# Thirteen modulation tiles folded on VectorE and moved to later stages, and a recurrence interleaved unit by unit

## The reference

```
m_x = silu(c) @ w_mod + b_mod            # six vectors of 1024: shift, scale, gate, shift, scale, gate
hx  = rmsnorm(x, g1) * (1 + m_x[1]) + m_x[0]
px  = hx @ w_in                           # columns rx, rg, u, v, gr, gg
xr  = dwconv1d(px.rx)                     # the same for the context
for direction in (forward, backward):     # bidirectional linear recurrence, 1280 channels
    r, i  = sigmoid(xr @ wa + ba), sigmoid(xr @ wx + bx)   # block-diagonal weights
    log_a = -8 * r * softplus(-lam);  a = exp(log_a)
    b     = sqrt(-expm1(2 * log_a)) * (i * xr)
    h_t   = a_t * h_(t-1) + b_t            # the context first, its last state starts the tokens
y_r = gelu(px.rg) * (h_fwd + h_bwd)
y_g = gelu(px.u) * (w_s @ rmsnorm(gelu(px.v)) + b_s)
x   = x + m_x[2] * ((sig(px.gr) * (y_r @ w_pr) + sig(px.gg) * (y_g @ w_pg)) @ w_out)
h2  = rmsnorm(x, g2) * (1 + m_x[4]) + m_x[3];  x = x + m_x[5] * conv_ffn(h2)
```

## Time and profile before

| | us |
|---|---|
| median of 3 runs | 3241.24 |
| lowest and highest | 3238.25, 3242.54 |
| profiled execution, its time | 3241.85 |
| its span, first to last instruction | 3240.0 |
| PE busy in the span | 3171.5 (98%) |
| DVE busy | 2060.2 (64%) |
| ACT busy | 1248.9 (39%) |
| mean granted TensorE clock | 0.993 |

### The profile page before, as it was taken

How to read it: one execution, slowest core, us unless ns; L and a number is a source line. 1 busy time by engine, 2 the same in 40 slices (tenths; PEclk the granted TensorE clock), 3 DMA queues, 4 the chain that set the end, 5 groups by cost and what they waited for, 6 DMA issues and landing times.

```text
span 3240.0 us, 37547 instructions
## 1 busy us (share of the span) xinstructions
PE 3171.5 (98%) x14084; PEld 2513.9 (78%) x14084; DVE 2060.2 (64%) x3455; ACT 1248.9 (39%) x2295; POOL 425.9 (13%) x186
## 2 busy tenths in 40 slices
PE   8999999999999999999999999999999999999999
PEld 7877778878778656767778888888888888888887
DVE  7678354367898899546646896777761455555554
ACT  4365222233223322235433335999982211111111
POOL 0000000014132000000002444333334000000000
PEclk9999999999999999999999999999999999999999
DMA  5243324332242454221122444676867555555553
GB/s 211 59 126 124 102 71 146 121 109 95 72 155 84 143 172 134 72 79 52 59 91 95 133 139 137 176 206 193 219 177 231 205 187 190 188 189 190 187 190 115
DMA packets 285845, 455.77 MB, mean 141 GB/s; under 512 B 148952, under 2 KB 156248, under 8 KB 285280
## 3 DMA queue, kind: packets, MB, share of 16 engines
q1 hardware_dynamic: 150560, 409.84, 37.9%
q10 hardware_dynamic: 135104, 43.52, 6.0%
HBM read 372.01 MB, written 81.26 MB: 140 GB/s over the span
## 4 chain that ended last, share of the span: by engine, by line
PE 91%; DVE 6%; ACT 1%; issue 1%; DMA 0%; POOL 0%; ACTq 0%; DVEq 0%
PE psum L644 91%; DVE wl L1489 1%; ACT wh L1077 1%; DVE yb L1701 0%; DVE psum L1865 0%; DVE trig L1584 0%; DVE lb L1692 0%; DVE st L1942 0%; DVE cs L1699 0%; DVE y L1703 0%; DVE trig L1587 0%; DVE trig L1586 0%; DVE trig L1589 0%; DVE trigw L1588 0%; DVE trigw L1585 0%
## 5 line engine op out<-in xcount | busy, mean ns | idle before, releaser
L644 PE MATMUL psum<-h_hi,wh 128*128 128x512 f32 x2144 | 857.0, 400 | 32.7 <-DVE h_lo L1633 13.2
L1489 DVE TENSOR_TENSOR wl<-ring,wh 128x1024 fp32r<-128x1024 f32 (+2 forms) x322 | 375.7, 1171 | 747.4 <-ACT wh L1077 746.4
L644 PE MATMUL psum<-h_lo,wh 128*128 128x512 f32 x2144 | 849.2, 396 | 0.0
L644 PE MATMUL psum<-h_hi,wl 128*128 128x512 f32 x2144 | 849.2, 396 | 0.0
L1077 ACT ACTIVATE wh<-ring 128x1024 fp32r<-128x1024 f32 (+2 forms) x492 | 504.6, 1027 | 813.5 <-PE psum L644 789.3
L2235 POOL TENSOR_TENSOR wl<-ring,wh 128x1024 fp32r<-128x1024 f32 x170 | 423.0, 2489 | 1784.3 <-ACT wh L1077 1784.3
L644 PEld LDWEIGHTS psum<-h_hi,wh 128*128 128x128 f32 x2144 | 406.4, 190 | 133.1 <-issue 40.6
L644 PEld LDWEIGHTS psum<-h_hi,wl 128*128 128x128 f32 x2144 | 405.8, 189 | 95.8
L644 PEld LDWEIGHTS psum<-h_lo,wh 128*128 128x128 f32 x2144 | 406.3, 190 | 88.5 <-issue 1.7
L644 PE MATMUL psum<-ews_hi,wh 128*128 128x512 f32 x1024 | 404.1, 395 | 0.7 <-ACT ga L1456 0.7
L644 PE MATMUL psum<-ews_hi,wl 128*128 128x512 f32 x1024 | 404.0, 395 | 0.0
(11 more groups left out here) (384 smaller groups left out, 3776.6 us busy)
## 6 DMA issues: line engine op xcount, KB each, us to landing
ring<-tables SPq DMA_DIRECT2D x256, 512.0 KB, 3.6
acts_scratch<-ga SPq DMA_DIRECT2D x128, 256.0 KB, 2.2
gates_scratch<-stage ACTq DMA_DIRECT2D x8, 4096.0 KB, 26.2
abuf<-acts_scratch SPq DMA_DIRECT2D x128, 256.0 KB, 3.8
gbuf<-gates_scratch SPq DMA_DIRECT2D x128, 256.0 KB, 4.0
ring<-w_up SPq DMA_DIRECT2D x44, 512.0 KB, 3.6
ring<-w_modb SPq DMA_DIRECT2D x32, 512.0 KB, 3.6
ring<-w_moda SPq DMA_DIRECT2D x16, 512.0 KB, 5.6
```

Of the source, the lines that this page charges most:

```text
L644: return nc.tensor.matmul(out, lhsT, rhs, start=first, stop=last, **kw)
L1489: TT(wl, slot(t, 0, size[t]), wh.bitcast(F32), ALU.subtract).then_inc(S("low_by_ve"), 1)
```

## The change

1. modb14 to modb26 leave the gates. They follow u0 to u6 and pg0 to pg5, one behind each (`FOLDED`). DVE folds each in its ring slot: it multiplies the 8 chunks by silu(c) and adds the chunks up in three steps (1024, 512, 256 and 128 columns), and PE does one matmul of the folded 128x128 chunk with ones, 16 columns, instead of eight. 14 tiles stay with the gates. The modulation of the second half (`a2`) is finished before the first `x_mixed`.
2. In the stages v, u, gg, map and pg, `high_after` and `low_after` look R = 5 tiles ahead instead of 3, at most three weight parts as before.
3. The recurrence: DVE's two steps for lq and la become one, in place (la = (la + 1) * lw, `loss_ready`), and ACT forms 1 - la (`decay_of`, Identity, 768 columns). DVE's groups are dissolved: after the scans of unit n come the last multiplication of unit n + 4 (`scale_input`) and the first two of unit n + 5 (`unit`).
4. Semaphores of the stage f and of iota are merged; no instruction of computation is added or removed there.

```diff
-MODB_LATE = 27
-MODB = [MODB_LATE * n // (2 * NR) for n in range(2 * NR + 1)]
+MODB_FOLD, MODB_LATE = 14, 27
+MODB = [MODB_FOLD * n // (2 * NR) for n in range(2 * NR + 1)]
+FOLDED = {f"u{n}": MODB_FOLD + n for n in range(7)} | {f"pg{n}": MODB_FOLD + 7 + n for n in range(6)}
...
+            def folded_modulation(name):
+                if name in FOLDED:
+                    k = FOLDED[name]
+                    pe.wait_ge(S("mod_folded"), k - MODB_FOLD + 1)
+                    mm(mods[:, k - MODB_FOLD, :], wchunk(TILE[f"modb{k}"], 0), ones[:, 0:MS], True, True)\
+                        .then_inc(PE, 1)
...
-            def high_after(t):
-                while next_high[0] < len(WHOLE_OF) and WHOLE_OF[next_high[0]] <= t + RH:
+            def high_after(t, ahead=RH):
+                while next_high[0] < len(WHOLE_OF) and WHOLE_OF[next_high[0]] <= t + ahead:
+                    if ahead > RH and WHOLE_OF[next_high[0] - RH] > t:
+                        break
...
+            def decay_of(n):
+                act.wait_ge(S("loss_ready"), n + 1)
+                A(la[:, n % 5, :], la[:, n % 5, :], ACT.Identity, scale=-1.0, bias=ones[:, 0:1])\
+                    .then_inc(S("a_ready"), 1)
...
+                if j:
+                    decay_of(n - 1)
                 wait(act, S("lru_done"), n - 4)
...
                 if j == 4:
+                    decay_of(n)
                     for k in range(5):
-                        act.wait_ge(S("a_ready"), n - 4 + k + 1)
+                        act.wait_ge(S("loss_ready"), n - 4 + k + 1)
                         A(lw[:, k, :], lw[:, k, :], ACT.Sqrt).then_inc(S("root"), 1)
...
+            def scale_input(n, j):
+                ve.wait_ge(S("a_ready"), n + 1)
+                ve.wait_ge(S("lru_in"), n + 1)
+                link(STT(lb[:, j, :], la[:, j, :], 1.0, lb[:, j, :], ALU.add, ALU.mult))
+            def unit(n, j):
+                ve.wait_ge(S("decay"), 2 * n + 2)
+                STT(la[:, j, :], la[:, j, :], 1.0, lw[:, j, :], ALU.add, ALU.mult).then_inc(S("loss_ready"), 1)
+                ve.wait_ge(S("gate_tanh"), 4 * n + 4)
+                STT(lb[:, j, :], ri[:, n % 2, :], 1.0, xr[:, c, :], ALU.add, ALU.mult).then_inc(S("lru_in"), 1)
...
+            for n in range(2 * NR):
+                scans(n, n % 5)
+                if 0 < n % 5 and n < 3 * 5:
+                    scale_input(n + 4, n % 5 - 1)
+                if n + 5 < 2 * NR:
+                    unit(n + 5, n % 5)
+                if n % 5 == 4 and n < 3 * 5:
+                    scale_input(n + 5, 4)
+                if n == 2 * NR - 7:
+                    low_after(TILE["rg0"] - RH)
+                if n == 2 * NR - 6:
+                    low_after(TILE["rg0"] - 1)
...
+            def fold_modulation(name):
+                if name in FOLDED:
+                    t = TILE[f"modb{FOLDED[name]}"]
+                    tile_here(ve, t)
+                    w = slot(t, 0, D).rearrange("p (c w) -> p c w", w=P)
+                    link(TT(w, w, silu_c.unsqueeze(2).to_broadcast([P, KD, P]), ALU.mult))
+                    for half in (4 * P, 2 * P):
+                        link(TT(slot(t, 0, half), slot(t, 0, half), slot(t, half, half), ALU.add))
+                    TT(wchunk(t, 0), wchunk(t, 0), wchunk(t, 1), ALU.add).then_inc(S("mod_folded"), 1)
...
             for n in range(NB + 1):
-                low_after(TILE[f"u{n}"])
+                fold_modulation(f"u{n + 1}")
+                low_after(TILE[f"u{n}"], R)
+                low_of_modulation(f"u{n}")
...
                 low_after(TILE[f"pr{n}"])
+                fold_modulation(f"pg{n}")
                 low_after(TILE[f"pr{n}"] + 1)
                 input_map(2 * n + 1)
```

More of the change, by code:

```diff
@@ L105 @@
     stage(f"pg{_u}", ["BT"], True, lambda k, u=_u: ("pg_mul", u + 1))
+    if f"pg{_u}" in FOLDED:
+        stage(f"modb{FOLDED[f'pg{_u}']}", ["T"], False)
 for _u in range(KD):
@@ L500, in _, with fetch_modulation @@
             stream("v", "w_v", 8)
-            stream("u", "w_u", HG)
+            def fetch_modulation(name):
+                if name in FOLDED:
+                    k = FOLDED[name]
+                    fetch(TILE[f"modb{k}"], io["w_modb"][k])
+            for u in range(HG):
+                fetch(TILE[f"u{u}"], io["w_u"][u])
+                fetch_modulation(f"u{u}")
             fetch(TILE["mix"], io["w_sT"])
@@ L1209, in _ @@
                     else:
-                        high_after(TILE[last])
+                        high_after(TILE[last], R)
+                        high_of_modulation(last)
             def squares(k, src, first, ready):
@@ L1489, in low, with low_after @@
                 TT(wl, slot(t, 0, size[t]), wh.bitcast(F32), ALU.subtract).then_inc(S("low_by_ve"), 1)
-            def low_after(t):
-                while next_low[0] < HALF[TILE["ui0"]] and WHOLE_OF[next_low[0]] <= t + RH:
+            def low_after(t, ahead=RH):
+                while next_low[0] < HALF[TILE["ui0"]] and WHOLE_OF[next_low[0]] <= t + ahead:
+                    if ahead > RH and WHOLE_OF[next_low[0] - RH] > t:
+                        break
                     if LOW[next_low[0]][0] == "low_by_ve":
@@ L1671, in _ @@
             ve.wait_ge(S("xr_ready"), NR)
[L1672 to L1686, removed]
-                    low_after(TILE["rg0"] - 1)
[L1688 to L1700, removed]
-                        link(v.tensor_tensor_scan(yb[:, ::-1], aj[:, 0:T][:, ::-1], bj[:, 0:T][:, ::-1],
-                                                  cs[:, 0:1], ALU.mult, ALU.add))
-                        TT(y[:, c, :], y[:, c, :], yb, ALU.add).then_inc(S("lru_done"), 1)
-                    if g == 3 and j in (1, 3):
-                        low_after(TILE[f"rg{j // 2}"])
@@ new lines, in scans @@
+            def scans(n, j):
+                c = n % NR
+                ve.wait_ge(S("root"), n + 1)
+                link(STT(lb[:, j, :], lb[:, j, :], 0.5, lw[:, j, :], ALU.mult, ALU.mult))
+                aj, bj = la[:, j, :], lb[:, j, :]
+                if n < NR:
+                    link(v.tensor_tensor_scan(cs, aj[:, T:TX], bj[:, T:TX], 0.0, ALU.mult, ALU.add))
+                    v.tensor_tensor_scan(y[:, c, :], aj[:, 0:T], bj[:, 0:T], cs[:, TC - 1:TC], ALU.mult,
+                                         ALU.add).then_inc(S("lru_done"), 1)
+                else:
+                    link(v.tensor_tensor_scan(cs[:, ::-1], aj[:, T:TX][:, ::-1], bj[:, T:TX][:, ::-1], 0.0,
+                                              ALU.mult, ALU.add))
+                    link(v.tensor_tensor_scan(yb[:, ::-1], aj[:, 0:T][:, ::-1], bj[:, 0:T][:, ::-1],
+                                              cs[:, 0:1], ALU.mult, ALU.add))
+                    TT(y[:, c, :], y[:, c, :], yb, ALU.add).then_inc(S("lru_done"), 1)
@@ new lines, in _ @@
+            for n in range(5):
+                unit(n, n)
+                if n:
+                    scale_input(n - 1, n - 1)
+            scale_input(4, 4)
+            for n in range(2 * NR):
[9 more added lines that the diff above has]
+                if n == 2 * NR - 6:
+                    low_after(TILE["rg0"] - 1)
+                if n in (2 * NR - 4, 2 * NR - 2):
+                    low_after(TILE[f"rg{(n - 2 * NR + 4) // 2}"])
```

69 lines of the change are left out of this document (48 added, 21 removed).

## The result

The changed kernel takes 3246.5 us in the median of 20 runs (3243.0 to 3247.9), the kernel before in the same rounds 3241.4 (3238.3 to 3244.6): a ratio of 1.0014, 95% interval 1.0008 to 1.0020. That is a slowdown of 5 us. It is clear of noise, but smaller than the 0.2% from which the chances count a change. The forecast was 3247. The profiled execution of the changed kernel, at 3247.9, was the slowest of its 20.

What follows compares the result with a forecast made beforehand. It took PE to bound the gates, with DVE's recurrence ending almost as late. Recurrence +2.5, folded matmuls +2.9, u6 fold +0.8 and round 0 -0.5 gave +5.7 us, stated as 3247; range 3234 to 3258.

Steps and rivals of the forecast that it cites:

- the term of the recurrence: Gates to rg5: the recurrence ends at 319.2 instead of 316.39, delaying rg5; +2.5 us, bounds -3 and +6.
- Tiles on PE: Thirteen tiles leave the gates, 22.6 us less PE work; 13 folded matmuls at 0.22 each return 2.9 us in later stages.
- The chain: Interleaved recurrence on DVE and ACT is a closed loop: steps 6.83 us forward, 7.56 backward, crossings between groups 12.3.
- the signs: What the profile should show: recurrence's last sum ending near 317 to 320, scans 6.8 and 7.6 us apart, gaps at crossings.
- the slow clock delays the next tanh by about 0.4: At each crossing in the gates, PE waits some 4 us or more; its slow clock then delays ACT's next tanh about 0.4.
- rg5: First matmul behind rg0 to rg4: done by about 321.5, rg5 starts near 324.7, with a wait and slow clock as before.
- Identity: ACT's new step forming 1 - la: 1.04 us without table load, bound 1.04 + 2.6; moving it hardly changes the sum.
- Folds: DVE folds take about 2.7 us each: +0.8 at u6, net -0.5 in round 0 with look-ahead, hidden in rounds 1 to 5.
- the rival of the folds: Late tiles or 4 us folds make rounds 1 to 5 and u2 to u6 wait about 1 us each: 3257; chance 0.12.
- PE's work: Sign over the whole kernel: PE's total of work falls by about 20 us, its idle time rises by more.
- The faster rival: Recurrence not a closed chain but following PE, rg5 starting at 292: 3213; needs `lw` before scans end; chance 0.12.
- The rival of the clock: PE idles at crossings and the slow level lasts through two following units each time: about +20, 3262; chance 0.12.

Runs made afterwards that it cites:

- e6: e1 with its 14 tiles placed at the crossings, 5, 5 and 4 behind gate units 5, 10 and 15; 3227.6 us, ratio 0.9945 to 0.9972.
- e7: Changed kernel with its 14 tiles placed at the crossings, 5, 5 and 4 behind units 5, 10 and 15; 3240.3 us, ratio 0.9991 to 1.0009.
- e3: Changed kernel, still interleaved, with both steps of la on DVE and no Identity on ACT; 3244.9 us, ratio 1.0001 to 1.0019.
- e2: Changed kernel with DVE's old groups, five units then five scans, Identity left on ACT; 3242.5 us, ratio 0.9997 to 1.0015.
- e11: e2 with the 14 tiles placed as in e6, so it differs from e6 by the Identity alone; 3236.3 us, ratio 0.9974 to 0.9992.
- e10: e9 with the 14 tiles moved: 4, 4, 4 and 2 behind units 5, 10, 15 and 17; 3222.9 us, ratio 0.9928 to 0.9955.
- e1: Changed kernel with the old recurrence (groups, both la steps on DVE), folds and look-ahead kept; 3236.9 us, ratio 0.9977 to 0.9995.
- e5: Kernel before with the wider look-ahead alone, all 27 tiles still in the gates; 3237.5 us, ratio 0.9977 to 0.9995.
- e9: e6 with one line more: DVE writes rg5's low part directly behind the last scans; 3224.2 us, ratio 0.9933 to 0.9960.

## Why the prediction was right, and where it was not

- **The time** was right, and partly by luck: the term of the recurrence was too small by 2.4 us, and two slow stretches behind waits, which I took to stay or hadn't thought of, were absent (-2.9). That they were absent is luck: behind the same wait of 3.29 us in round 0 e6 has its slow stretch (last section).
- **Tiles on PE.** Folded matmuls 13 x 0.24 = 3.1 against 2.9. Right.
- **The chain.** Steps of 6.82 and 7.55 against 6.83 and 7.56, crossings of 12.18 against 12.3. Right, and e7 shows that it is a chain: filled with tiles, PE's waits vanish or shrink, and the step stays. Two steps of the third group take 6.95 in the changed kernel, PE's own pace for a unit and a tile, as PE is late there behind the slow clock; in e7 they are 6.82 too. The recurrence ended at 322.8, later than the "317 to 320" of the signs.
- **What failed in size: "the slow clock delays the next tanh by about 0.4".** It was 1.5 and 1.6 us at the first two crossings (8.59 and 8.44 against 7.07 and 6.82 in e7) and 0.7 at the third (8.25 against 7.54): 3.8 in place of 1.2, which covers what the term was short by (4.9 against 2.5). I took the loss from a row where 1.30 us of idleness cost PE 1.7; behind 3.76 and 6.90 us it was 3.0 (13.49 for two units instead of 10.5) and 2.8 (8.19 for one instead of 5.4), and the tanh of the next unit waits for the slow unit.
- **rg5.** It waited 1.71 us, where the forecast has about 3.2 (324.7 - 321.5). "A wait and a slow clock in front of rg5 as before" was half wrong: the clock stayed up.
- **Identity.** 0.94 us and no table load, against 1.04; this agrees with the Trainium skill, ScalarE: Activation LUTs, on table sets. I said that the move hardly changes the sum. Interleaved that holds (1.6 us, e3); in groups it costs 5.6 (e2) to 8.8 (e11). The Trainium skill's advice against simple arithmetic on ScalarE (Trainium Architecture — The Big Picture, the five engines) has the right sign here: the Identity takes 0.94, DVE's own step 0.56. But most of what it costs in groups is its place in ACT's program, as e11 shows, and not these 0.4 us.
- **Folds.** 2.7 us each (1.22, 1.15 and 0.29, and the links), the wait at u6 0.53 against 0.8 (the forecast's own terms, 6.7 + 2.74 + 2.7, give 12.1 and not 12.4, so 0.5), round 0 3.29 against about 3.1, none in rounds 1 to 5. Right; the rival of the folds falls.
- **PE's work** was to fall by about 20 us and its idle time to rise by more. PE's busy time fell by 10.9 (3171.5 to 3160.6), since matmuls on the slow clock count as busy for longer, and its idle time rose by 17.0.
- **The faster rival** falls by e7. The condition that I gave it was right: it needs `lw` before the scans end, which the groups have and the interleaving gives up.
- **The rival of the clock**: its mechanism was there, at 0.7 to 1.6 us for each crossing and not 7. The Trainium skill, TensorE: Matmul & The Clock Gate, on oscillation, has waits between bursts make each burst start slow. The traces agree for the fourteen longest waits in the gates (3.75 to 8.38 us, all runs together), and not for every shorter one (below).
- **What the prediction didn't ask** was where the tiles go that stay. I costed 14 x 1.74 on PE wherever they lay. Placed at the crossings they cost next to nothing (e6 to e10), and their place is worth more (9.4 us, e1 to e6) than the whole change costs.

## What to carry to other kernels

Interleaving shortened nothing here, because the step that follows needs the buffer that the step before frees. Write down the closed loop and its length before dissolving a group, since the group may be what lets the other engine run ahead. Work that is taken off the busiest engine comes back as waits unless what remains is moved to where that engine would wait anyway; look where its waits are, and put the movable work there, but count the slots that it takes from the next stage's fetches. An instruction moved to a less busy engine costs its place in that engine's order, which can be more than its duration.

## What the runs showed of the hardware that I had not expected

- **The slow level behind a wait is not fixed by the wait.** At the same unit and after the same 1.30 us, the gates took 7.09 in the kernel before and 5.40 in e5. In front of rg5 three kernels wait 3.26 to 3.28 us. In e11 the matmuls are slow at once, in e2 none of the first 20 is, and in e6 the first five run at full speed, and from 307.3 on seven take 0.63 each. So the duration of the first matmul doesn't tell; the windows do. First matmul of e11 and of e2, then windows of PE in e2 and in e6 (columns as in the earlier trace rows):

```profile
313.10 0.77 PE L658 MATMUL psum<-h_hi,wh 128*128 128x512 f32 x1 [3.27 <-DVE wl L1532]
...
320.69 0.47 PE L657 MATMUL psum<-h_hi,wh 128*128 128x512 f32 x1 [3.26 <-DVE wl L1531]
...
320.70:326.00 5.30, 5.30 (x23) 1.00 0.63 170
...
307.30:310.60 3.30, 3.30 (x10) 0.50 0.56 185
```

- What it costs is not fixed either. In round 0 PE waits 3.29 us in the changed kernel, 3.29 in e6 and 3.30 in e9; from that transposition to the next one it is 11.60, 14.34 and 13.05 us, so the slow level costs nothing, 2.7 and 1.5.
- The scatter between runs of one kernel goes with the mean clock. Eleven runs of e2: two at a mean clock of 0.989 take 3247.9 us on average, two at 0.992 take 3238.9; in e5 two runs at 0.991 take 3240.4 and the one at 0.995 takes 3232.7. What decides whether a given wait is followed by the slow level stays open.
- A matmul with 16 columns between two projections costs 0.24 us, a whole tile of 8 with 64 columns 1.74, so 0.22 each. At these widths the count of instructions, and not the columns, sets the price of such tiles.
